# A mixture-of-experts stage: gate and up weights requested ahead of down, and VectorE's weight copy placed behind the gated product

## The reference, cut to what matters

```python
scores = jax.nn.sigmoid(hf @ w_router)
...
_, eidx = lax.top_k(jnp.where(emask, choice, -jnp.inf), TOP_K)      # 8 of 128 experts for each row
...
def expert_block(args):
    tok, rw, e = args
    xs = hp[tok]
    y = swiglu(xs, w_gate_e[e], w_up_e[e], w_down_e[e])              # (silu(xs@wg) * (xs@wu)) @ wd
    return (y * rw[:, None])
...
routed = jnp.zeros((T + 1, D)).at[row_tok].add(y.reshape(R, D))[:T]
return routed + shared
```

## Time and profile before

| | us |
|---|---|
| median of three runs | 3116.49 |
| lowest, highest | 3113.28, 3119.24 |
| the profiled execution | 3119.66 |
| its span, first to last instruction | 3117.6 |

### The profile page before, as it was taken

One profiled execution on the slowest core, in us unless ns is written; L12 is line 12 of the kernel. 1 busy time (PEld: TensorE's weight loads), 2 busy tenths in 40 slices (PEclk: granted clock), 3 DMA queues, 4 the chain that ended last, 5 costly groups with the idle time before them and its releaser, 6 DMA issues.

```text
span 3117.6 us, 45745 instructions
## 1 busy us (share of the span) xinstructions
PE 2847.7 (91%) x12896; PEld 1243.8 (40%) x12897; DVE 1428.9 (46%) x2398; ACT 817.8 (26%) x1255; POOL 729.2 (23%) x461
## 2 busy tenths in 40 slices
PE   5789999999979999999999989999999999998780
PEld 2355555555544433333333333333333333333230
DVE  1146666676664244444433434444344444443345
ACT  0033333333320122222222222222222222222124
POOL 0001101101112023333322323322233223232220
PEclk9899999999989999999999989999999999999895
DMA  9711111111135377689999988899899997878848
GB/s 375 241 42 55 54 61 44 64 49 52 61 114 180 108 232 229 192 250 303 307 313 320 320 293 271 269 345 308 312 290 327 299 302 240 283 227 299 298 129 330
DMA packets 150818, 684.92 MB, mean 220 GB/s; under 512 B 26433, under 2 KB 27074, under 8 KB 100866
## 3 DMA queue, kind: packets, MB, share of 16 engines
q1 hardware_dynamic: 100194, 533.08, 45.2%
q0 software_dynamic: 50592, 151.43, 21.0%
HBM read 574.20 MB, written 128.06 MB: 225 GB/s over the span
## 4 chain that ended last, share of the span: by engine, by line
PE 76%; DMA 10%; DVE 8%; issue 3%; ACT 2%; SPq 1%; DVEq 0%; ACTq 0%; POOLq 0%
PE PB L1220 30%; PE PB L1227 17%; PE PB L1124 9%; DMA arena<-in_w_up_e 7%; PE PB L1094 5%; PE PB L1048 3%; PE PB L1040 2%; PE PB L1071 2%; DMA arena<-in_ada_b 2%; PE PB L1185 1%; PE PB L1233 1%; PE PB L1151 1%; PE PB L1108 1%; DMA arena<-acc_tab 1%; DVE arena L886 1%
## 5 line engine op out<-in xcount | busy, mean ns | idle before, releaser
L1220 PE MATMUL PB<-arena 128*64 x2544 | 1123.2, 595 | 1.1 <-DVE arena L961 1.1
L1221 PE MATMUL PB<-arena 128*64 128x512 f32 x2544 | 1123.2, 595 | 0.0
L528 POOL DMA_INDIRECT acc_tab<-arena,rec x158 | 426.3, 2698 | 1305.1 <-DMA acc_tab<-arena,rec 633.9
L1220 PEld LDWEIGHTS PB<-arena 128*64 128x64 f32 x2544 | 350.6, 138 | 737.1 <-issue 737.1
L1228 PE MATMUL PB<-arena 128*64 128x512 f32 x1264 | 617.8, 612 | 0.0
L1227 PE MATMUL PB<-arena 128*64 x1264 | 617.7, 612 | 0.0
L958 DVE COPY arena<-arena 128x4096 f32 x161 | 369.4, 2295 | 201.2 <-DMA arena<-in_w_up_e 139.2
L994 DVE SCALAR_TENSOR_TENSOR arena<-PB,RW,G 128x512 f32<-128x512 f32 x316 | 222.7, 746 | 291.0 <-PE PB L1228 282.5
L1221 PEld LDWEIGHTS PB<-arena 128*64 128x64 f32 x2544 | 351.0, 138 | 0.0
L486 POOL DMA_INDIRECT rec_tab<-recs,posi x128 | 124.1, 969 | 844.9 <-DVE recs L816 803.6
L641 ACT COPY arena<-arena 128x2048 f32 x159 | 300.5, 1890 | 0.7 <-issue 0.7
(11 more groups left out here) (237 smaller groups left out, 2182.3 us busy)
## 6 DMA issues: line engine op xcount, KB each, us to landing
arena<-in_w_gate_e SPq DMA_DIRECT2D x128, 1024.0 KB
arena<-in_w_up_e SPq DMA_DIRECT2D x128, 1024.0 KB, 10.5
arena<-in_w_down_e SPq DMA_DIRECT2D x128, 1024.0 KB, 6.5
arena<-in_ada_w SPq DMA_DIRECT2D x12, 2048.0 KB, 12.6
arena<-in_x SPq DMA_DIRECT2D x32, 512.0 KB, 3.6
acc_tab<-arena SPq DMA_DIRECT2D x32, 512.0 KB, 2.6
arena<-acc_tab SPq DMA_DIRECT2D x6, 2048.0 KB, 22.1
h_tab<-arena SPq DMA_DIRECT2D x16, 512.0 KB, 2.9
```

The costliest lines, as they stand in the source:

```text
L528: g.indirect_dma_start(acc_tab, bass.IndirectOffsetOnAxis(ap=rec[:, n, 1:2], axis=0), ys[n % 2], None, compute_op=ALU.add).then_inc(s["add ...
L1220: mm(B[7][0:SUB, :], xTm[:, k, 0:SUB], wa(k), start=(k == 0), stop=(k == KD - 1))
L1221: last = mm(B[7][SUB:P, :], xTm[:, k, SUB:P], WBG[n % 2][:, k], start=(k == 0), stop=(k == KD - 1))
```

## The change

SyncE's order of requests: gate and up of expert e now come ahead of down of expert e-1, and down e-1 waits for the unit that freed its own slot (`w`). Before it was gate e, up e, down e. The first four experts of the loop (4 to 7) are written out, since the loop carries `w` over. Down 3 now comes after gate and up 4. VectorE's copy for the second sub-block is made one pass later in count: `gu_copy` for unit b+2 stands in pass b between the gated product and the lower rows' copy, where before `gu_copy` for unit b+3 stood at the pass's end, and the third copy ahead of the loop is gone. At the end SyncE waits for one copy less.

```diff
             gate_up_after(3, 3)
-            down_after(3, 3)
             sp.wait_ge(s["e_tab"], 1)
-            with sp.Fori(1, E // SLOTS) as q:
+            def freed(sem, u):
+                sp.wait_ge(s[sem], u)
+                settle(sp)
...
+            for e in range(SLOTS, 2 * SLOTS):
+                u = last_unit(e - SLOTS)
+                freed("gu_done", u)
+                gate_up_after(e % SLOTS, e)
+                if e > SLOTS:
+                    freed("y_done", w)
+                down_after((e - 1) % SLOTS, e - 1)
+                w = u
+            with sp.Fori(2, E // SLOTS) as q:
                 for n in range(SLOTS):
...
                     gate_up(n, e)
-                    sp.wait_ge(s["w_d"], e * 16 + 16)
+                    if n == 0:
+                        w = sp.value_load(tab[0:1, bass.ds(e + (6 * P - 5), 1)], min_val=1, max_val=MAXU)
+                    sp.wait_ge(s["w_d"], e * 16)
                     settle(sp)
-                    sp.wait_ge(s["y_done"], u)
+                    sp.wait_ge(s["y_done"], w)
                     settle(sp)
-                    down(n, e)
+                    down((n - 1) % SLOTS, e - 1)
+                    w = u
+            w = last_unit(E - 1 - SLOTS)
+            freed("y_done", w)
+            down_after(SLOTS - 1, E - 1)
...
-            sp.wait_ge(s["v_cg"], nu + 3)
+            sp.wait_ge(s["v_cg"], nu + 2)
...
             rows_lower()
-            gu_copy(2, 2)
...
                             v.wait_ge(s["eg_done"], b + 2)
                             gated()
+                            gu_copy(n, v.snap(b + 2))
                             v.wait_ge(s["xg_used"], b + 3)
                             rows_lower()
...
-                            gu_copy(n + 1, v.snap(b + 3))
```

More of the change, by code:

```diff
@@ L430, in _, with last_unit @@
             gate_up_after(3, 3)
-            down_after(3, 3)
             sp.wait_ge(s["e_tab"], 1)
-            with sp.Fori(1, E // SLOTS) as q:
+            def freed(sem, u):
+                sp.wait_ge(s[sem], u)
+                settle(sp)
+            def last_unit(e):
+                at = tab[0:1, 6 * P + e:6 * P + e + 1] if isinstance(e, int) else tab[0:1, bass.ds(e + 6 * P, 1)]
+                return sp.value_load(at, min_val=1, max_val=MAXU)
+            for e in range(SLOTS, 2 * SLOTS):
[7 more added lines that the diff above has]
+            with sp.Fori(2, E // SLOTS) as q:
                 for n in range(SLOTS):
```

## The result

The changed kernel takes 3156.73 us (median of four, 3152.41 to 3159.37) beside 3117.64 for the kernel before: ratio 1.0126, 95% interval 1.0109 to 1.0144. The forecast was 3057, 2% faster, in a range of 3038 to 3094. The profiled execution took 3157.57 us, its span is 3155.6.

The account below looks back on a forecast made before the run. TensorE sets the time at 11.693 us per unit, interrupted by 86.7 us of stalls for late weights. 3119.66 - 86.7 + 3 + 10 + 8 + 6 = 3060, against the median 3057 us; range 3038 to 3094.

Parts of the forecast that it names:

- The stalls and the order: SyncE's weight requests: gates held behind down products cause 86.7 us of stalls; the new order leaves 3 and 10 us.
- the walk: Gate request times worked out expert by expert and unit by unit at 11.5 us per expert; gate 33 at 1599.7.
- Rivals 2 and 3: Weight transfers: 2, bandwidth, earlier requests only queue, 3078 at half, chance 0.13; 3, landing binds, no effect, 3113 to 3119, 0.03.
- VectorE between two gate/up products: The copy now precedes the lower rows in every unit; 0.09 us spare, price 0.05 us per unit, 8 us in all.
- the gap before the copy: VectorE, between the gated product's end and the weight copy: assumed 0.46 us; 0.6 would use up the spare.
- Rival 1: VectorE's per-unit chain outgrows its cover: 0.15 to 0.3 us per unit, 24 to 47 us, 3073 to 3096; chance 0.17.
- Rival 4: POOL ahead of VectorE's copy in most units, copy and later work wait: slower, 3167 at 0.7 us per unit; chance 0.05.
- That scatters get faster: POOL's scatters, now mostly issued away from VectorE's copy, take 1.58 us to issue instead of 3.36.
- the 6 us for collisions: Late POOL scatters or gathers being issued when VectorE's copy wants to start: one in six of 77 at 0.5 us.
- Down later: Down weights land some 16 us after their expert's up; ScalarE's copy needs them 21 us on, so 0 us, end 10.

Follow-up runs that it names:

- the kernel with the loads ahead: The changed kernel with both register loads of the weight copy (ring place, landing count) moved ahead of VectorE's wait for the silu: 3043.55 us, ratio 0.9743.
- The kernel with one load behind the product: The changed kernel with only the ring place's load moved ahead of the silu wait, the landing count's load staying behind the gated product: 3054.96 us, ratio 0.9774.

## Why the prediction was wrong

**The stalls and the order: right.** Where they were, what held the gates, and that the new order frees them: the order alone gave 3048. In the kernel with the loads ahead gate 33 went at 1599.98, where the walk had 1599.7; nothing was lost in units 43 to 62 (taken as 3) nor at 90 (0), and 8.5 us in unit 153 (10, with the restart), 11.0 when it was run again. In the 8.5 us TensorE stood 6.8; the rest came after the restart, at a granted clock of 0.5. Rivals 2 and 3 fall with it: that kernel shows what the transfers allow.

**The step that failed** is "VectorE between two gate/up products", and in it the term "the gap before the copy is 0.46 now, behind a short instruction; no row shows it behind this one", with 0.05 us per unit and 8 us in the sum. It was 0.79 us and 123 us. The gap was taken for a hand-over of fixed length. It was what two register loads had left over, behind longer instructions than the gated product. Behind a product of 0.61 us 1.16 stick out: the 0.70 us more, less the 0.09 that were spare, make 0.61. Another 0.10 is the hand-over: the lower rows end at 1577.62 and TensorE begins at 1577.86, 0.24 us, where the forecast allowed just the 0.14 of the weight load (1569.08 - 1568.94). That gives 0.71 us, and the product is 0.70 late in this unit. The last 0.08 of the 0.79 are spread over the unit, as in the first matmuls of the product, 0.48 us apart instead of 0.43, and why isn't shown. The kernel with one load behind the product bears the path out: its gap is that of the forecast, and so nearly is its time. Two warnings stood in the text. The spare was 0.09 us against a price paid 157 times, and the upper end of 0.3 us was no bound worked out from a row. The kernel before had such a row, of VectorE's sequencer at the first of the two loads, that wasn't read:

```profile
L952 DVEq TENSOR_LOAD <-cst x161: 300/307/558, 1055.0 to 3036.4; - x161
```

Two loads of 0.31 us each alone are longer than 0.46, so most of them must have lain beside other work. **Rival 1**, the per-unit chain that outgrows its cover, is what happened, and the sign that the forecast gave for it came: a wait of TensorE before the gate/up product in each unit. It had a chance of 0.17, but didn't name the loads and ended at 0.3 us per unit and so on the faster side. 0.79 is above the 0.55 us that use up 86.7 us of stalls, and the sign turned there.

**Rival 4**, POOL ahead of the copy, fell: in the changed kernel every scatter is issued in 1.57 to 1.63 us, and no copy takes more than 2.30. That scatters get faster was right; the 6 us for collisions were not there.

**Down later: right.** ScalarE's copy of the down weights never waited for them: its 159 instructions have 0.7 us of idle time ahead of them in all, put down to issue.

## What to carry to other kernels

When an instruction is moved, move on paper all that its engine's sequencer does for it: register loads from a tensor took 0.65 us each here, and a gap in the timeline shows only what its neighbours didn't cover. Load registers ahead of the wait in which the engine stands idle. And when a step enters a chain that every unit runs through, compare its slack with its uncertainty times the number of units: 0.09 us of slack times 157 decided over a gain of 87 us. Test the parts of such a change apart; here one was worth 2.4% and the other took more than that back.

## What the runs showed of the hardware

VectorE's sequencer goes on while its datapath works: the loads began 0.1 us after the start of the gated product (1573.07 against 1572.96). With the loads gone from there the copy starts 0.45 us after the product's start (1588.96 against 1588.51), so before the product's end, with two semaphore waits between them. The two waits and the copy's own preparation take 0.36 us of the sequencer behind the loads (1574.37 to 1574.73). Behind a running instruction of 0.61 us that is covered and costs nothing; a register load costs its full time as soon as the sequencer outlasts the instruction. The sequencer can be more than one instruction ahead: in the kernel before it began the first load at 1558.2, when the second output row (1558.57) and the small copy (1559.23), which come ahead of it in the program, hadn't begun.

TensorE's granted clock fell to 0.5 at each of the nine waits of 4.9 to 8.9 us, and in no unit of the changed kernel, with waits of at most 1.1 us.

Moving the weight copy away from the output rows made POOL's scatters shorter to issue: 2.70 us on average before and 3.06 with the order alone, 1.58 in the changed kernel, with the copy alone, and with the new order and both loads ahead. POOL's wait for the last scatter to land is another matter and doesn't go by the copy alone: 633.9 us in 77 waits before, 170.4 in 21 with the order alone, 231.4 in 24 with the copy alone, 89.1 in 10 with the order, the later copy and the loads ahead, 29.8 in 3 in the changed kernel. It isn't a steady measure either: the kernel with 89.1 had 28.2 in 3 when it was run again. VectorE waits for scatters as well, 59.5 us in 35 waits with the order alone beside 8.5 in 5 before. What all this costs is within the microseconds left open above.
